# Expert biases added on VectorE from block-transposed columns instead of by products on TensorE

## What is computed

```python
xt = h.reshape(T, D)                               # T = 512 tokens, D = 1024
logits = (xt @ router_w + router_b)
top_v, top_i = lax.top_k(logits, TOP_K)            # 4 of 32 experts for a token
gate = jax.nn.softmax(top_v, axis=-1)
...
def expert_block(args):
    xb, e = args
    hc = xb @ w1[e] + b1[e]                        # w1[e]: 1024 x 2048, b1[e]: 2048
    gt = jnp.minimum(hc[:, :D_FF], SWIGLU_LIMIT)
    up = jnp.clip(hc[:, D_FF:], -SWIGLU_LIMIT, SWIGLU_LIMIT)
    glu = gt * jax.nn.sigmoid(SWIGLU_ALPHA * gt)
    return ((up + 1.0) * glu) @ w2[e] + b2[e]      # w2[e]: 1024 x 1024, b2[e]: 1024
...
y = y * buf_w[:, None].astype(y.dtype)             # the token's gate
out = jnp.zeros((T + 1, D), y.dtype).at[buf_tok].add(y)[:T]
```

## Time and profile before

| | us |
|---|---|
| median of three executions | 1576.27 |
| lowest, highest | 1574.11, 1576.81 |
| span of the profiled execution, first to last instruction | 1572.2 |
| expert stage in it (first to last product of the experts) | 533.6 to 1548.6 |
| busy in it: PE, PEld, VectorE, ScalarE, GpSimd | 1531.1, 646.5, 509.8, 248.4, 312.2 |
| moved over the span | 468.17 MB, mean 298 GB/s |

### The profile page before, as it was taken

The page is one execution under the profiler, slowest core; times in us unless marked ns, Lnnn a source line. Parts: engine busy times, 40 slices in busy tenths (PEclk is TensorE's granted clock), DMA queues, the critical chain, the costliest instruction groups (busy, mean ns, idle before and its releaser), DMA issues.

```text
span 1572.2 us, 31271 instructions
## 1 busy us (share of the span) xinstructions
PE 1531.1 (97%) x13047; PEld 646.5 (41%) x13048; DVE 509.8 (32%) x940; ACT 248.4 (16%) x510; POOL 312.2 (20%) x449
## 2 busy tenths in 40 slices
PE   7999999999999999999999999999999999999994
PEld 4654555665445633333333333333333333333331
DVE  4104555242325542233223322332233222322232
ACT  4213443232422100000000000000000000010001
POOL 2000002442200202122212221222122212222111
PEclk9999999999999999999999999999999999999997
DMA  9122130520261699999999999999999999999995
GB/s 239 27 57 52 40 80 25 174 80 27 70 265 54 259 383 401 409 415 414 413 408 414 415 413 408 413 415 413 407 415 413 414 407 414 415 415 409 410 417 196
DMA packets 108446, 468.17 MB, mean 298 GB/s; under 512 B 29591, under 2 KB 71615, under 8 KB 83794
## 3 DMA queue, kind: packets, MB, share of 16 engines
q1 hardware_dynamic: 94610, 446.55, 70.3%
q0 software_dynamic: 13792, 21.00, 6.1%
HBM read 452.41 MB, written 19.29 MB: 300 GB/s over the span
## 4 chain that ended last, share of the span: by engine, by line
PE 83%; DMA 13%; DVE 2%; ACT 1%; issue 1%; DVEq 0%; PEld 0%; SPq 0%; POOL 0%; POOLq 0%; PEldq 0%; ACTq 0%
PE ps L1689 35%; PE ps L1278 12%; DMA ring<-in_expert_w 12%; PE ps L1708 11%; PE ps L1428 7%; PE ps L1716 5%; PE ps L1618 4%; PE ps L1413 2%; PE ps L1390 2%; PE ps L1400 2%; ACT mixT L1076 1%; PE ps L1568 0%; DMA ring<-x 0%; PE ps L1680 0%; PE ps L1698 0%
## 5 line engine op out<-in xcount | busy, mean ns | idle before, releaser
L1689 PE MATMUL ps<-ring,oT_fox 128*32 128x512 f32 x6096 | 662.3, 592 | 3.2 <-DMA ring<-in_expert_w 3.2
L1689 PEld LDWEIGHTS ps<-ring,oT_fox 128*32 128x32 f32 x6096 | 201.0, 110 | 443.3 <-issue 419.2
L2291 DVE TENSOR_TENSOR mixT<-ps,mask 128x768 f32<-128x768 f32 x64 | 60.9, 952 | 679.9 <-PE ps L1689 679.9
L1708 PE MATMUL ps<-ring,hT 128*32 128x512 f32 x2048 | 266.3, 592 | 0.0
L1716 PE MATMUL ps<-ring,hT 128*32 128x256 f32 x2048 | 156.8, 379 | 0.0
L1428 PE MATMUL ps<-hT,ring 128*128 128x512 f32 x304 | 137.0, 597 | 0.0
L1716 PEld LDWEIGHTS ps<-ring,hT 128*32 128x32 f32 x2048 | 68.0, 110 | 148.8 <-issue 147.6
L1202 ACT ACTIVATE mixT<-mixT 128x768 f32<-128x768 f32 x32 | 27.0, 845 | 618.0 <-DVE mixT L2295 618.0
L887 POOL DMA_INDIRECT oT_nsa<-table,pc x93 | 100.2, 1077 | 47.2 <-POOL pc L882 28.0
L1278 PE MATMUL ps<-hT,ring 128*128 128x512 f32 x208 | 92.1, 602 | 0.2 <-ACT hT L1006 0.2
L882 POOL COPY pc<-pc 128x3 int32 (+1 forms) x31 | 5.9, 191 | 421.0 <-DMA x<-hT,v_win 390.8
(11 more groups left out here) (308 smaller groups left out, 1138.8 us busy)
## 6 DMA issues: line engine op xcount, KB each, us to landing
ring<-in_expert_w SPq DMA_DIRECT2D x191, 2048.0 KB, 20.0
ring<-in_w_in SPq DMA_DIRECT2D x28, 512.0 KB, 4.8
ring<-in_w_out SPq DMA_DIRECT2D x8, 512.0 KB, 8.9
ring<-in_w_in SPq DMA_DIRECT2D x1, 2144.0 KB, 12.8
xs<-in_x SPq DMA_DIRECT2D x4, 512.0 KB, 5.0
ring<-in_w_in SPq DMA_DIRECT2D x8, 256.0 KB, 3.5
ring<-in_w_proj_nsa SPq DMA_DIRECT2D x16, 128.0 KB, 2.8
ring<-in_w_proj_fox SPq DMA_DIRECT2D x8, 256.0 KB, 3.1
```

What stands on the lines that cost most here:

```text
L1689: ins = pe.matmul(wide(ps[TG * j:TG * j + TG, hc + g, :]), xT[b][:, g, c, :], up_slab(slots[c // 2], c % 2, j), start=(c == 0), stop=(c == ...
L1708: ins = pe.matmul(ps[TG * q:TG * q + TG, bank, :], gT[b][:, q // 2, c, :], rows[:, at:at + 512], start=False, stop=(c == NK - 1), tile_pos ...
L2291: return dve.tensor_tensor(to, half, b_up[:, 256 * n:256 * n + 256].unsqueeze(1).broadcast_to([P, NG, 256]), ALU.add)
```

## The change

The products with `pick` and `bias` go, and with them the three-part split, `pick`, its copies on GpSimd, and ACT's copy of the first bias out of PSUM. Instead:

- SP loads both biases raw, in float32, into `b_rows` (`pT`, 128 partitions by 1280 elements), by 12 transfers of 655 KB in all, each block of 32 partitions with the columns that its tile needs. They wait for `pT_free` and stand ahead of the loop of `load_mix`.
- VectorE turns them once by one 128x1280 transpose in blocks of 32x32, in the mix stage (`turn_bias`). An expert's bias is then a column for each 32 output columns.
- For each expert VectorE copies the 16 columns of the first bias, and transposes them, repeated 32 times, to 128x512 (`spread_up`); and in the same way 24 columns to 128x768 for the second bias (`spread_down`).
- The second product starts its own sum (`start=(c == 0)`), and VectorE adds the second bias to it out of PSUM (`sum_y`), before ACT multiplies by the gate. ACT waits for `y_summed` in place of `w2_used`.
- For the last expert VectorE multiplies the bias by the gate ahead of time and does the gate, the add and the way out of PSUM in one instruction for each part (`last_y`), in place of ACT.
- The first load of expert weights (`load_pair(0, 0)`) waits for a product of the last attention step instead of `bias_ready`. PE no longer waits for `bias_ready`, `consts2`, `pick_up_ready` and `pick_down_ready`.

```diff
-            def split_bias(c):
+            def spread_up(e, at):
+
+                dve.tensor_copy(up_now, bias_of(e, 0, UP_B)).then_inc(up_taken, 1)
+                dve.wait_ge(up_taken, at + 1)
+                dve.transpose(blocks(b_up), up_now.broadcast_to([P, UP_B // TG, TG])).then_inc(b_up_ready, 1)
+
+            def spread_down(e, at):
+
+                dve.tensor_copy(down_now, bias_of(e, UP_B, DOWN_B)).then_inc(down_taken, 1)
+                dve.wait_ge(down_taken, at + 1)
+                dve.transpose(blocks(b_down), down_now.broadcast_to([P, DOWN_B // TG, TG])).then_inc(b_down_ready, 1)
+
+            def turn_bias(c):
 
                 if c == 2:
...
+                    dve.wait_ge(b_loaded, 16 * 12)
+                    dve.transpose(blocks(b_cols), blocks(b_rows)).then_inc(bias_turned, 1)
                 elif c == 4:
...
+                    dve.wait_ge(bias_turned, 1)
+                    spread_up(0, 0)
...
+            def sum_y(e):
+
+                spread_down(e, e)
+                dve.wait_ge(b_down_ready, e + 1)
+                dve.wait_ge(w2_used, 4 * e + 4)
+                dve.tensor_tensor(b_down, y_ps, b_down, ALU.add).then_inc(y_summed, 1)
+
+            def last_y():
+
+                dve.wait_ge(y_ready, E - 1)
+                spread_down(E - 1, E - 1)
+                dve.wait_ge(b_down_ready, E)
+                for n, cols in enumerate((slice(0, 512), slice(512, 768))):
+                    dve.tensor_scalar(b_last[n], b_down[:, cols], gate_y[:, n, E - 1:E], None, ALU.mult).then_inc(b_last_ready, 1)
+                dve.wait_ge(b_last_ready, 2)
+                dve.wait_ge(y_stored[1], 32 * (E // 2 - 1))
+                for n, (cols, signal) in enumerate(((slice(0, 512), y_half_ready), (slice(512, 768), y_ready))):
+                    dve.wait_ge(w2_used, 4 * E - 3 + n)
+                    dve.scalar_tensor_tensor(yb[1][:, cols], y_last[:, cols], gate_y[:, n, E - 1:E], b_last[n],
+                                             ALU.mult, ALU.add).then_inc(signal, 1)
...
             expert(0, 0, None)
+            spread_up(1, 1)
             after_first()
             with dve.Fori(0, E // 2 - 1) as i:
-                expert(2 * i + 1, 1, gather * i + gather + 16)
-                expert(2 * i + 2, 0, gather * i + 2 * gather)
+                for b, e, landed in ((1, 2 * i + 1, gather * i + gather + 16), (0, 2 * i + 2, gather * i + 2 * gather)):
+                    expert(e, b, landed)
+                    spread_up(e + 1, e + 1)
+                    sum_y(e - 1)
             expert(E - 1, 1, None)
+            sum_y(E - 2)
+            last_y()
...
             def take_y(e, b, k):
 
-                act.wait_ge(w2_used, 4 * e + 4)
+                act.wait_ge(y_summed, e + 1)
...
-            def up_bias(b):
...
-            def down_bias(b, at=Y_BANK):
...
-                pe.wait_ge(pick_down_ready, e + 1)
                 down(b, W2_SLOTS, lambda s: pe.wait_ge(slabs_loaded[(NK + s) // 2], 16 * e + 16) if s % 2 == 0 else None,
...
-            b, n = Fills(N_FOX_LAST, FOX_LAST)("gf")
-            sp.wait_ge(work_full[b], n + 1)
-            sp.dma_start(b_raw[1], expert_b2[0]).then_inc(b_loaded, 16)
+            sp.wait_ge(pT_free, 3 * PAIRS + 1)
+            for q in range(4):
+                rows = b_rows[TG * q:TG * q + TG, :]
+                sp.dma_start(rows[:, 0:UP_B].rearrange("e (n m) -> e n m", n=2),
+                             expert_b1[0].rearrange("e (n j m) -> j e n m", n=2, j=4)[q]).then_inc(b_loaded, 16)
+                sp.dma_start(rows[:, UP_B:UP_B + 512], expert_b2[0][:, q % 2 * 512:q % 2 * 512 + 512]).then_inc(b_loaded, 16)
+                sp.dma_start(rows[:, UP_B + 512:], expert_b2[0][:, 256 * q:256 * q + 256]).then_inc(b_loaded, 16)
```

More of the change, by code:

```diff
@@ L426, in hybrid_block, with bias_of, blocks @@
         b_up = mask[:, :]
+        def bias_of(e, first, n):
+            col = b_cols[:, first:first + n].rearrange("p (k e) -> p k e", e=E)
+            return col[:, :, e:e + 1] if isinstance(e, int) else col[:, :, bass.ds(e, 1)]
+        now_b = cmp_one[:, :, :, :].rearrange("p a b c -> p (a b c)")
+        up_now, down_now = (now_b[:, 32 * n:32 * n + w // TG].unsqueeze(2) for n, w in enumerate((UP_B, DOWN_B)))
+        def blocks(v):
+            return v.rearrange("p (k m) -> p k m", m=TG)
         xs_f = xs[:, :, :].rearrange("p t d -> p (t d)")
@@ L860, in _ @@
             pool.wait_ge(consts2, 4)
-            pool.memset(pick, 1.0).then_inc(consts2, 1)
-            for j in range(3):
-                part = pick[E * j:E * (j + 1), :, :]
-                pool.wait_ge(consts2, 5 + j)
-                pool.affine_select(out=part, in_=part, compare_op=ALU.is_equal, fill=0.0, base=0,
-                                   pattern=[[-1, E], [0, TG]], channel_multiplier=1).then_inc(consts2, 1)
-            pool.wait_ge(consts2, 8)
             for t in range(NT):
@@ L907, in scattered_halves @@
                                         in_=yb[b][:, 0:512], in_offset=None, compute_op=ALU.add).then_inc(y_stored[b], 16)
-            def picked(to, e, b, signal):
-                row = pick[:, e, :] if isinstance(e, int) else pick[:, bass.ds(e, 1), :].rearrange("p a m -> p (a m)")
-                pool.tensor_copy(to[:, b, :], row).then_inc(signal, 1)
-            picked(pick_up, 0, 0, pick_up_ready)
-            for b in range(2):
-                picked(pick_down, b, b, pick_down_ready)
             pool.wait_ge(idx_ready, 2)
@@ L1191, in _ @@
                     act.activation(expd[:, t, :], expd[:, t, :], ACT.Exp).then_inc(expd_ready, 1)
-            def take_b_up(e):
-                act.wait_ge(w1_used, NK * e + 1)
-                if isinstance(e, int) and e == 1:
-                    act.wait_ge(hc_free, 1)
-                act.activation(b_up, ps[:, NG, :], ACT.Copy).then_inc(b_up_ready, 1)
             def sigmoid(e):
@@ L1221, in _ @@
                 for b in range(2):
-                    take_b_up(2 * i + b + 3)
                     sigmoid(2 * i + b + 3)
                     take_y(2 * i + b + 2, b, i + 1)
-            take_b_up(E - 1)
             sigmoid(E - 1)
             take_y(E - 2, 0, E // 2 - 1)
-            act.wait_ge(y_stored[1], 32 * (E // 2 - 1))
-            for n, (cols, signal) in enumerate(((slice(0, 512), y_half_ready), (slice(512, 768), y_ready))):
-                act.wait_ge(w2_used, 4 * E - 3 + n)
-                act.activation(yb[1][:, cols], y_last[:, cols], ACT.Copy, scale=gate_y[:, n, E - 1:E]).then_inc(signal, 1)
             act.wait_ge(extra_ready, 1)
@@ L1239, in _ @@
                         act.wait_ge(y_stored[b], 32 * E // 2)
[L1240 to L1242 removed]
+                    act.wait_ge(ov_dve, 4 * o + 2)
                     act.activation(sg_b, gt_b, ACT.Sigmoid, scale=ALPHA).then_inc(ov_act, 1)
[L1244 removed]
+                    act.wait_ge(ov_dve, 4 * o + 4)
                     act.wait_ge(ov_over, o + 1)
@@ L1674, in wide @@
                 return c.rearrange("p (n m) -> p n m", n=2)
-            def up_bias(b):
-                for j in range(4):
-                    cols = bias[:, 0:2 * F].rearrange("p (n j m) -> p n j m", n=2, j=4)[:, :, j, :]
-                    pe.matmul(wide(ps[TG * j:TG * j + TG, NG, :]), pick_up[:, b, :], cols, start=True, stop=True,
-                              tile_position=(0, TG * j))
             def up(b, slots, loaded, used, hc=HC):
@@ L1692, in up @@
                     used(c, ins)
-            def down_bias(b, at=Y_BANK):
-                for q in range(4):
-                    n = q % 2
-                    pe.matmul(ps[TG * q:TG * q + TG, at, :], pick_down[:, b, :], bias[:, 2 * F + n * 512:2 * F + (n + 1) * 512],
-                              start=True, stop=False, tile_position=(0, TG * q))
-                for q in range(4):
-                    pe.matmul(ps[TG * q:TG * q + TG, at + 1, 0:256], pick_down[:, b, :], bias[:, 2 * F + q * 256:2 * F + (q + 1) * 256],
-                              start=True, stop=False, tile_position=(0, TG * q))
             def down_halves(b, c, rows, bank=Y_BANK):
@@ L1748, in expert @@
                 if isinstance(e, int) and e == 1:
-                    pe.wait_ge(b_up_ready, 1)
                     pe.wait_ge(rows_ready, 1)
@@ L2383, in _ @@
                     turn_act(0).then_inc(ov_dve, 1)
+                    dve.wait_ge(ov_pe, 5 * o + 5)
+                    dve.wait_ge(b_down_ready, E + o + 1)
+                    dve.tensor_tensor(b_down, y_ps, b_down, ALU.add).then_inc(ov_dve, 1)
             def means(n):
```

87 lines of the change are left out of this document (22 added, 65 removed).

## The result

| | before | after |
|---|---|---|
| median of nine executions on one chip, us | 1575.02 | 1579.77 |
| lowest to highest | 1574.03 to 1576.81 | 1578.51 to 1581.97 |
| span of the profiled execution | 1572.2 | 1577.6 |
| VectorE's first instruction on the summed rows | 1560.40 | 1565.75 |

The changed kernel is slower: ratio 1.0029, interval 1.0019 to 1.0038, some 4.7 us. The prediction was 1575.6 us with a range up to 1578.2, so it was wrong, and on the side that it had given 7%. It had been added to the median of three executions of before, 1576.27 us; nine give 1575.02. So the plain comparison is that of the differences: 0.65 us less was forecast, 4.7 us more was measured.

The account below looks back on a forecast made before the run. Loads of weights at 412 GB/s were taken as the bound, PE living on a lead. Only the hole in down(0) counted: 1576.27 - 0.65 = 1575.6 us, all other terms 0; range 1572.6 to 1578.2 us.

Parts of the forecast that it names:

- the side that it had given 7%: The whole kernel slower by more than a measurement can tell from no change, above 1579.4 us: chance 0.07.
- The end: Result's path after the last expert: the add's 1.0 us offset by PE's gains, worth 0; bound if it fails +0.7 us.
- Products taken from PE: Expert stage: bias products removed save PE 0.55 us per expert, 17.6 us in all, worth 0 where DMA engines are full.
- The arriving saving: Rival: PE sets the pace in the expert stage, so 17.6 us would go, giving 1558.7 us; chance 5%.
- The hole in down(0): First expert's down product, DMA engines run dry: the gap ends 0.65 us earlier, and all later loads with it; -0.65 us.
- VectorE in the loop: Expert loop: 4.0 us of added VectorE work per expert, 13 us of 32 in all, nothing waits for it; 0.
- The result's path in the loop: Expert loop: y reaches ACT and the scatter 1.0 us later, against some 26 us of cover; 0.
- The lead is worth more: Rival: PE, earlier with each expert, fills further thin spots in the loads; 1574.6 us, chance 7%.
- The loads run slower: Rival in the expert loop: VectorE's added work and later scatter lower the DMA rate; 407 GB/s would give 1587.9 us; 6%.
- The handover of the chain: Expert stage: the chain of waits goes over from PE to the loads of weights near 1000 us instead of 1270 us.
- GpSimd's lock at the end: Rival: VectorE's SBUF multiplications for the last expert delay GpSimd's scatter of y(30) by 0.56 us; 1576.2 us, chance 12%.
- Mix stage: Before the experts: the bias transfers, the 2.7 us transpose and the removed split delay nothing; 0.

Follow-up runs that it names:

- the first experiment: The changed kernel with one outer condition (total > 0) on VectorE around its 21 empty turns for overfull experts: 1575.67 us, ratio 1.0002.

## Why the prediction was wrong, point by point

**The step that failed: "The end".** It followed the result from `last_y` through GpSimd's scatter, and counted VectorE's last instruction in place of ACT's, "0". It never asked what stands *behind* `last_y` in VectorE's own program. That is 21 empty turns and then the normalisation, which the whole program waits for. The move of the last evacuation from ACT to VectorE put a wait for PE's last product ahead of them. Their price is 3.9 us: the first rows' landing let ACT start at 1560.59 us. The rows that VectorE takes land some 1.3 us behind these (in the first experiment ACT started at 1559.87 and VectorE, waiting for its rows, at 1561.14), so it could have started at about 1561.85: 1565.75 - 1561.85 = 3.9. The experiment that takes the turns out gives back 4.1 us, and the one with more turns adds theirs in full.

Most of this could have been read ahead of the run. The row of before's instruction on the summed rows says that VectorE was idle for 26.43 us; 11 of these were the turns. An idle time of 26 us that holds sequencer work is no cover of 26 us. Each turn also became longer, from 0.53 to 0.70 us, with the larger body that it jumps over; that could not have been read from before.

**The rest of the 5.4 us between the spans, 1.5 us, isn't shown to be the change's.** In after's profiled execution 1.2 us of it had run up ahead of the last quarters: the experts' first product on weights came at 534.62 us, 533.90 in before, and PE got the last piece of weights at 1542.74, against 1541.54 in the earlier trace rows. In the pair without turns the same bias work has the last quarters out at 1549.92 us and a span of 1572.2, that of before, while the kernel of before with its turns held back, without the bias change, sent them at 1552.72. Single executions differ by this much, and nothing here tells a small cost of the change from that.

**Products taken from PE: right.** Worth 0 beside full DMA engines: leaving them out altogether gives 1575.09 against 1575.02 us. The 0.55 us each were right too, by the pair with shorter loads. PE's wait for the last piece grew as forecast, from 0.89 to 1.46 us in the pair without turns. *The arriving saving* (5%) is thereby refuted for this kernel, and shown to be what happens with shorter loads.

**The hole in down(0), the whole of the -0.65 us: right in size at its place, not seen at the end.** PE gets there 0.55 us earlier, as counted. But the last piece of weights doesn't come earlier for it. From the experts' first product on weights to PE's start on that piece it is 1007.7 to 1008.1 us in four traces with the new bias work (after, the two with turns jumped over and the one with more turns) and 1007.3 to 1008.9 in four with the old. Why the 0.55 us are lost on the way was not tried. By the medians it can't be told: the pair with all turns jumped over has them 1.25 us apart in the other direction, the pair with VectorE's alone 0.3 us apart in this one, with intervals of 1.4 us to each side.

**VectorE in the loop: right that it costs nothing, too high in its terms.** The new work of one expert in after, 1000 to 1032.2 us, below a transpose that was there before and is shown for its price (count, busy us, mean ns, idle before):

```profile
L2225 DVE STREAM_TRANSPOSE hT<-mixT 128x768 f32<-128x768 f32 x1 | 1.6, 1607 | 0.0
L2018 DVE STREAM_TRANSPOSE pT<-cmp_one 128x768 f32<-128x768 f32 x1 | 1.0, 979 | 0.0
...
L2265 DVE TENSOR_TENSOR pT<-ps,pT 128x768 f32<-128x768 f32 x1 | 1.0, 958 | 0.1
...
L2012 DVE STREAM_TRANSPOSE mask<-cmp_one 128x512 f32<-128x512 f32 x1 | 0.7, 712 | 0.0
...
L2016 DVE COPY cmp_one<-pT 128x24 f32 x1 | 0.1, 142 | 0.0
L2010 DVE COPY cmp_one<-pT 128x16 f32 x1 | 0.1, 133 | 0.0
```

The five new ones take 2.9 us together, not 4.0. The transposes had been costed by the same shape at 1.59 us; that shape was right and its access pattern wasn't (below).

**The result's path in the loop: right.** Nothing on the path there waited for y; the rate and the pitch of the loads were the same. *The lead is worth more* (7%) did not come: without any product of the biases the kernel was no faster. At the end of the experts the path came out level by its slack, as the pair without turns shows, and not by the gains on PE of 0.65 and 0.5 us that had been set against the add. *The loads run slower* (6%) had the right sign and the wrong mechanism: the rate stayed at 412 GB/s.

**The handover of the chain: "near 1000 us", measured 954.73.** The term was counted to the moment at which PE first waits. The chain goes over where that load was *issued*, a load's 26.3 us earlier. About 992 - 26 = 966 us would have been the sum. The same holds for before: 600 + 22 x 31.5 is 1293 us, the chain changes hands at 1270, and a load of 26 us lies between.

**GpSimd's lock at the end: it did not come.** VectorE's first multiplication within SBUF fell right under GpSimd's issue of the scatter of y(30) (1542.18 and 1541.71 us, above), and that issue took 1.58 us as against 1.57 for the halves of y(31) in the earlier trace rows. The Trainium skill (SBUF — State Buffer, SBUF: two separate sides) has whichever of the two starts first hold the pair of ports for its whole instruction, which the prediction had left out; GpSimd had started first. By that rule the 0.56 us that the prediction put on GpSimd could not have come, and if anyone was held it was VectorE. Its 128x512 multiplication took 0.82 us there, and one of the same shape, elsewhere in this trace, 0.53:

```profile
L1918 DVE TENSOR_SCALAR mixT<-mixT,st 128x512 f32<-128x512 f32 x12 | 6.3, 529 | 0.0
```

It ended at 1543.00 us, before GpSimd did (1543.29), so it wasn't held for the whole issue, and there the trace doesn't bear the rule out. No run here isolates what made it longer.

**Mix stage: right.** Nothing of it shows in the time: the experts' first product on weights comes between 533.51 and 534.74 us in the five kernels with the new mix stage and between 533.90 and 536.06 in the six with the old.

## What to carry to other kernels

When the last step of a path moves to another engine, read the program of that engine *behind* it to its end, sequencer work included: loops whose turns are empty are no rows of busy time, but they run in order, and a wait that is put ahead of them uncovers them. One test ahead of a loop that is mostly empty (`If(total > 0)`) cost nothing that could be measured here (1575.97 against 1576.03 us) and takes the turns out of such a wait when there is nothing to do. And a saving on an engine that lives on a lead over the loads was worth nothing here, however busy the page calls it; shorten the loads before you believe that the work itself was free.

## What the runs showed of the hardware

- **Empty turns of three loops took 0.26, 0.53 and 0.70 us, longer with a larger body.** On VectorE's sequencer the loop's own register and branch instructions take 36 to 72 ns each, yet a turn took 0.26 us with one instruction in its body, 0.53 us in before and 0.70 us in after. The place doesn't make the difference: held back in before, a turn still took 0.53 us, and behind the added loop after's still took 0.70. Which part of the larger body makes it longer was not tried.
- **Block transposes of one shape differed by the access pattern of their source.** 128x768 took 1607 ns where the source is read with a stride (`turn_act`, `take_x`), and 979 ns from a repeated column; 128x512 took 712 ns. The mix stage's transpose of 128x1280, from contiguous columns, took less than the strided one of 128x768:

```profile
L2024 DVE STREAM_TRANSPOSE pT<-pT 128x1280 f32<-128x1280 f32 x1 | 1.5, 1502 | 0.0
```

  (979 - 712) / 256 = 1.04 ns a column and (1502 - 979) / 512 = 1.02 ns agree, with 0.18 us to start. So a repeated column costs no more than contiguous ones, and the strided reading of 128x768 took 0.6 us more. The source's pattern is what differs in the program; no run changed it alone.
- **PE's busy time hides short pauses.** Without the products PE was busy 8.1 us less where the loads pace it (1531.6 to 1523.5 us) and 18.0 us less where PE paces itself (1529.5 to 1511.5, the two kernels with shorter loads). A product is recorded with 593 ns, but 192 of them follow each other in 20.60 us, 107 ns apart; so, by these figures, the records of the last ones run on into a pause and cover its first half microsecond. The same pause in weight loading and in the products, after's bias work with all turns jumped over:

```profile
1541.49 0.16 PEld L1649 LDWEIGHTS ps<-ring,hT 128*32 128x32 f32 x8 [1.46 <-DMA ring<-in_expert_w]
1541.49 3.64 PE L1649 MATMUL ps<-ring,hT 128*32 128x512 f32 x32 [0.55 <-DMA ring<-in_expert_w]
```

  Whoever looks for a wait on PE reads the weight loading's rows (which show 0.27 to 0.30 us between loads even where nothing is waited for).
